# PEER block: the sums of gathered `u` rows written straight into the table of dots

## The reference, cut to what matters

```python
def block(args):
    xb, eb, gb = args
    u = u_tab[eb]
    act = jax.nn.gelu(jnp.einsum('thkd,td->thk', u, xb), approximate=False)
    return jnp.einsum('thk,thkd->td', gb * act, v_tab[eb])
```

## Time and profile before

| | |
|---|---|
| time, median of 3 runs | 2834.77 us (2832.07 to 2835.41) |
| span of the profiled execution | 2830.4 us |
| median less this span | 4.4 us |
| TensorE busy | 2757.7 us (97%) |
| VectorE busy | 2169.3 us (77%) |
| ScalarE busy | 1115.4 us (39%) |
| GpSimd busy | 1628.8 us (58%) |
| mean granted TensorE clock | 0.993 |

### The profile page before, as it was taken

The page is one execution under the profiler, slowest core; times in us unless marked ns, Lnnn a source line. Parts: engine busy times, 40 slices in busy tenths (PEclk is TensorE's granted clock), DMA queues, the critical chain, the costliest instruction groups (busy, mean ns, idle before and its releaser), DMA issues. The chain is left out here.

```text
span 2830.4 us, 47325 instructions
## 1 busy us (share of the span) xinstructions
PE 2757.7 (97%) x16000; PEld 1508.1 (53%) x16000; DVE 2169.3 (77%) x4268; ACT 1115.4 (39%) x1554; POOL 1628.8 (58%) x1485
## 2 busy tenths in 40 slices
PE   6999999999999999999999999999999999999998
PEld 3445754554666666656666665444444444444443
DVE  3998865322788999989999994777777777777778
ACT  4354554223444444446677664312211221222122
POOL 1331001111233444477777775888888898889884
PEclk9999999999999999999999999999999999999999
DMA  3231030111344555568888888899999999999995
GB/s 128 79 137 35 1 139 22 58 47 42 110 156 162 191 192 185 177 238 308 321 308 308 322 307 321 316 367 330 338 343 339 328 343 358 352 343 352 358 349 189
DMA packets 265252, 658.08 MB, mean 233 GB/s; under 512 B 17552, under 2 KB 116112, under 8 KB 261952
## 3 DMA queue, kind: packets, MB, share of 16 engines
q1 hardware_dynamic: 190992, 387.37, 38.2%
q0 software_dynamic: 74160, 269.52, 26.7%
HBM read 547.24 MB, written 110.10 MB: 232 GB/s over the span
## 5 line engine op out<-in xcount | busy, mean ns | idle before, releaser
L95 POOL TENSOR_TENSOR w_low<-w_ring,w_high 128x1024 f16<-128x1024 f32 x164 | 375.3, 2289 | 884.9 <-ACT w_ring L90 884.3
L1605 PE MATMUL psum<-region_y,w_high 128*128 128x384 f16 x2048 | 670.4, 327 | 10.8 <-issue 4.3
L1606 PE MATMUL psum<-region_y,w_high 128*128 128x384 f16 x2048 | 670.5, 327 | 0.0
L1607 PE MATMUL psum<-region_y,w_low 128*128 128x384 f16 x2048 | 670.4, 327 | 0.0
L2320 DVE TENSOR_TENSOR region_x<-region_x,psum 128x1024 f32<-128x1024 f32 x192 | 234.3, 1220 | 213.6 <-PE psum L2154 213.4
L2171 ACT ACTIVATE scores<-w_ring 128x1024 bf16<-128x1024 f32 x64 | 67.0, 1048 | 655.6 <-PE psum L2154 651.6
L2152 PE MATMUL psum<-scores,share 128*128 128x512 bf16 x752 | 286.0, 380 | 7.7 <-DVE region_x L2320 6.9
L2152 PE MATMUL psum<-scores,wh 128*128 128x512 bf16 x768 | 291.2, 379 | 1.4 <-POOL wl L2203 1.4
L2154 PE MATMUL psum<-scores,wl 128*128 128x512 bf16 x768 | 291.2, 379 | 0.0
L2153 PE MATMUL psum<-vl,wh 128*128 128x512 bf16 x768 | 291.2, 379 | 0.0
L1663 ACT ACTIVATE ge<-psum 128x384 f32<-128x384 f32 x256 | 124.9, 488 | 415.6 <-PE psum L1607 413.5
(11 more groups left out here) (306 smaller groups left out, 5478.3 us busy)
## 6 DMA issues: line engine op xcount, KB each, us to landing
w_ring<-in_u_t_dram SPq DMA_DIRECT2D x128, 512.0 KB, 6.1
acts_dram<-ge SPq DMA_DIRECT2D x128, 384.0 KB, 4.8
gates_dram<-scores SPq DMA_DIRECT2D x24, 2048.0 KB, 9.2
scores<-gates_dram SPq DMA_DIRECT2D x30, 1536.0 KB, 16.4
scores<-acts_dram SPq DMA_DIRECT2D x30, 1536.0 KB, 19.8
w_ring<-in_v_t_dram SPq DMA_DIRECT2D x64, 512.0 KB, 11.0
more_v<-in_v_t_dram SPq DMA_DIRECT2D x64, 512.0 KB, 4.9
w_ring<-in_w_stream_dram SPq DMA_DIRECT2D x20, 512.0 KB, 3.5
```

The lines of the kernel that those rows point to most:

```text
L95: pool.tensor_tensor(self.wl[:, s, :], self.wf[:, s, :], self.wh[:, s, :], ALU.subtract).then_inc(self.w_lo, 1)
L1605: pe.matmul(a, uh[:, par, row], xh[:, n, cols], start=(n == 0), stop=False)
L1606: pe.matmul(a, uh[:, par, row], xl[:, n, cols], start=False, stop=False)
L1607: last = pe.matmul(a, ul[:, par, row], xh[:, n, cols], start=False, stop=(n == KC - 1))
```

## The change

A take's sum now goes straight to its column in `dot`, in both stages. The small tables `dots`, the copies out of them, and the semaphore `dot_ok` with all its waits are gone. Who waited for `dot_ok` waits for something else: ScalarE at the switch for `row_used`, SyncE's load of `final_g` for `acc_ok`.

```diff
             def take(group, slot, seen, tile):
-                after(dve, dot_ok, group)
                 dve.wait_ge(row_in[slot], seen)
                 for j in range(SLOT_ROWS):
                     a = row[slot * SLOT_ROWS + j]
                     dve.scalar_tensor_tensor(out=a, in0=a, scalar=1.0, in1=xtok[tile], op0=ALU.mult, op1=ALU.mult,
-                                             accum_out=dots[:, j:j + 1]).then_inc(row_used, 1)
-                dve.wait_ge(row_used, SLOT_ROWS * group + SLOT_ROWS)
-                dve.tensor_copy(dot[:, tile, ds(SLOT_ROWS * group - SEL * tile, SLOT_ROWS)],
-                                dots[:, :]).then_inc(dot_ok, 1)
+                                             accum_out=dot[:, tile, ds(SLOT_ROWS * group + (j - SEL * tile), 1)]
+                                             ).then_inc(row_used, 1)
...
-            sp.wait_ge(dot_ok, GROUPS // 2)
+            sp.wait_ge(acc_ok, 3)
             sp.dma_start(xtok[:, :], final_g).then_inc(xtok_in, 16)
...
                     if at_switch(g) and (what, c) == ("v", CPG - 1):
-                        act.wait_ge(dot_ok, PHASE)
+                        act.wait_ge(row_used, used(PHASE, True))
                         act.activation(dot[:, 1, :], dot[:, 1, :], ACT.Gelu, scale=1.0 / XS).then_inc(gelu_ok, 1)
...
                 if kind == "u":
                     dve.scalar_tensor_tensor(out=row[j], in0=row[j], scalar=1.0, in1=acc[1], op0=ALU.mult,
-                                             op1=ALU.mult, accum_out=dots[:, k:k + 1]).then_inc(row_used, 1)
-                    if k == U_ONE - 1:
-                        dve.wait_ge(row_used, used(g, True) + U_ONE)
-                        dve.tensor_copy(dot[:, 1, ds(U_ONE * g + U_DONE, U_ONE)], dots[:, :]).then_inc(dot_ok, 1)
+                                             op1=ALU.mult, accum_out=dot[:, 1, ds(U_ONE * g + (U_DONE + k), 1)]
+                                             ).then_inc(row_used, 1)
...
             def add(g, of_u):
-                if of_u:
-                    after(dve, dot_ok, g)
                 for q in range(PAIRS):
```

More of the change, by code:

```diff
@@ L1462, in select_and_activate @@
     step_rows = sb(ctx, "u_step_rows", [P, RING, SLOT_ROWS], I32)
-    dots = sb(ctx, "u_dots", [P, SLOT_ROWS], F32)
     zero = sb(ctx, "u_zero", [P, 1], F32)
@@ L1467, in select_and_activate @@
     tok_in = sems("u_tok_in")
-    zero_ok, step_ok, row_used, dot_ok = (sems(f"u_{n}") for n in (
-        "zero_ok", "step_ok", "row_used", "dot_ok"))
+    zero_ok, step_ok, row_used = (sems(f"u_{n}") for n in ("zero_ok", "step_ok", "row_used"))
     rest = work[:, 0:HP * NK].rearrange("p (h n) -> p h n", h=HP)
@@ L2019, in combine @@
     step_rows = sb(ctx, "step_rows", [P, 2, BOTH], I32)
-    dots = sb(ctx, "dots", [P, U_ONE], F32)
     weight = sb(ctx, "weight", [P, GATHERED, SEL], F32)
@@ L2030, in combine @@
     row_in = [sems(f"row_in{j}") for j in range(BOTH)]
-    xtok_in, zero_ok, step_ok, row_used, dot_ok, gelu_ok, weight_ok, acc_ok = (sems(n) for n in (
-        "xtok_in", "zero_ok", "step_ok", "row_used", "dot_ok", "gelu_ok", "weight_ok", "acc_ok"))
+    xtok_in, zero_ok, step_ok, row_used, gelu_ok, weight_ok, acc_ok = (sems(n) for n in (
+        "xtok_in", "zero_ok", "step_ok", "row_used", "gelu_ok", "weight_ok", "acc_ok"))
     TILES = [*range(GATHERED, TB - 1), *range(GATHERED), TB - 1]
```

## The result

The changed kernel takes 2843.0 us (median of 5 runs, 2840.4 to 2846.2), the kernel before beside it 2833.4 us: a ratio of 1.0043, 95% interval 1.0032 to 1.0054. It is **slower by 9.6 us**; the prediction said 2844.1 us and +9.3. The profiled spans differ by 10.8 us, 2841.2 against 2830.4.

The account below looks back on a forecast made before the run. TensorE, busy 97% of the span, was taken as the bound, with GpSimd the second chain. Terms -0.5 - 0.2 + 8.0 + 2.0 = +9.3 us; 2839.7 + 4.4 gave 2844.1 us, range 2838 to 2849.

Parts of the forecast that it names:

- The switch, +8.0 and +2.0: Start of group 16: TensorE waits behind Gelu's later wait, +8.0 us, then loses +2.0 us at the low clock.
- Group 0 to 2, -0.2: Combine's start: group 0 ends 7.3 us earlier, but TensorE waits 5.1 us for GpSimd at group 2, clock 2.0: -0.2 us.
- Selection, -0.5: Selection stage: dropping 88 copies may shorten TensorE's wait for GpSimd at 1223 to 1227: -0.5 us, at most 6.7.
- The second half: From group 20: groups of 31.45 instead of 31.08 us cost 4.1 us; recurrence left open, 0 in the sum.
- rival (a): No change: clock stays up at both new waits, or second-half slide stays away; +5.3 or +5.2 us; chance 0.24.
- Rival (c): Slower still: GpSimd stays the bound from the switch, with longer low clock and slow additions; +12.8 us, chance 0.12.
- Rival (b): Faster: without copies GpSimd is early at 1223, groups 0 to 2 and the second half; -8.1 us, chance 0.04.

Follow-up runs that it names:

- the early Gelu: Changed kernel with ScalarE's Gelu at the switch waiting for the fifth take of group 15 (row_used 155), not the tenth: 2831.7 us, ratio 1.0003.
- The two runs with GpSimd's order: GpSimd's eight subtractions before its gathers in groups 2 to 5; changed kernel with Gelu waiting for row_used 155: 2826.4 us; kernel before: ratio 1.0003.
- the run of that part alone: Kernel before with the 88 copies of the selection stage left out and combine untouched: ratio 1.0003.
- GpSimd's small addition: Changed kernel, Gelu waiting for row_used 155, one of GpSimd's five small additions per group from group 1 on left out: 2826.2 us, ratio 0.9984.
- the maximum: Kernel before, with combine's copy of the dots written as a two-input maximum of the table with itself: ratio 0.9996.

## Why the prediction was right

The terms that carry the sum came out where and as predicted, but part of the nearness of +9.6 to +9.3 is luck: without the selection the terms add up to +9.8 against 9.73 in the inner length, with 1.05 us too little at the switch and 1.1 us too little gain in groups 0 to 2.

*The switch, +8.0 and +2.0.* Right in place, chain and size: 8.75 and 2.30. Five runs that change only where or for what the Gelu waits move it as the chain says: 0 for the fifth take, the eighth, and the Gelu placed behind; 4.3 for the ninth; 10.3 for the tenth, in the kernel before (waits and low clock together). ScalarE's idle time was 26.02 us where some 26 had been expected. Of the 0.75 that was missing, 0.5 is the pair of subtractions: I took 4.1 us, between 3.7 and 5.3, and it took 4.64 (2324.16 to 2328.80), beside a weighting that itself took 6.93 us.

*Group 0 to 2, -0.2.* Right in mechanism: group 0 -7.66 for -7.3, GpSimd's start of group 2 at 1860.07 for 1859.7, the wait of TensorE +4.97 for +5.1, the clock +1.36 for +2.0. That nets to -1.33 in the changed kernel's profile, not -0.2; more than half of the difference is the low clock, which varies by a microsecond between profiles. With the early Gelu the whole inner length shows -0.02. The two runs with GpSimd's order show both halves to be real.

*Selection, -0.5.* Its sign isn't shown. Group 0 starts 1.10 us later in the changed kernel's profile, but the profile was already 1.35 us behind at 705 us (a matmul at 704.31 before, at 705.66 after), ahead of the changed lines, and the run of that part alone shows no difference.

*The second half.* Right (0): the groups of 31.45 us are back, and they begin with one late gather, as the prediction read it. What it left open, whether that happens again, the profiles settle: the gather is late in all twelve that have GpSimd's small addition, whatever happens at the switch. So the single event was no ground for the weight that rival (a) took from it. Rival (c), GpSimd the bound from the switch on, did not come: TensorE's group 16, 2.3 us longer at the low clock, gave time to GpSimd, which was 2.96 us ahead at the start of group 17 and 0.76 at that of group 18, as in the kernel before. Of its terms the rows show the slower subtractions and 0.3 us of the longer low clock.

*Rival (b)* asked for a GpSimd that the copies held up. In group 0 the trace has it the other way round: GpSimd's subtractions ran at 2.11 to 2.14 and 1.62 to 1.65 us while the copy waited. By the Trainium skill (SBUF — State Buffer, Who interferes with whom) the first to issue keeps the shared ports for a whole instruction. The direction agrees with these rows. The length doesn't: the copy waited through five subtractions that began after it, and so did the maximum, which the Trainium skill counts as contending for its two SBUF inputs. Near 1227 a wait of TensorE did shrink without the copies, from 3.81 to 1.07 us, and came back as 3.39 at 1245.8, so that nothing measurable was gained there.

## What to carry to other kernels

When a signal is replaced by a count on another semaphore, work out which instruction gives that count and what that instruction waits for: here "all ten takes" instead of "the first five" tied a ScalarE wait to the end of TensorE's own group, with TensorE's next inputs queued behind it. Put an instruction that waits for something late behind whatever others need soon. And before a stall is booked as a gain, ask which other engine is late by as much; removing VectorE's stall alone gave 0 to 1.4 us, reordering GpSimd alone 0.2, and both 7.7 us.

## What the runs showed of the hardware

A VectorE operation of 128x5 elements with all its operands in SBUF waited 10.46 us through GpSimd's back-to-back subtractions, and 3.11 us when the run was parted. Copy or two-input maximum made no difference. Takes and adds with an input in PSUM ran beside the same subtractions at their usual 1.2 us. The four weightings of a group (768 columns each, both inputs in SBUF by the code), which met two subtractions in the changed kernel at the switch, took 6.93 us together instead of 3.56, and all of that is in the last two, which otherwise take 0.95 us each:

```profile
2324.43 2.88 DVE L317 TENSOR_TENSOR scores<-scores 128x768 f32<-128x768 f32 x1
```
```profile
2327.23 2.39 DVE L317 TENSOR_TENSOR scores<-scores 128x768 f32<-128x768 f32 x1
```

Each ends 0.8 us behind a subtraction (these end at 2326.5 and 2328.8), as if it had been held until then; and the second subtraction, which starts while the third weighting is still to be done, takes 2.34 us instead of 1.64. So a weighting got in between two subtractions that follow each other at once, where the small copy did not in a run of six. By what the copy was held across instructions, no run here tells.

The cost of the low clock (1.2 GHz) after a wait of TensorE hardly follows the wait: 1.7 us after 2.6 us of waiting, 1.3 to 2.6 us after 4.4 to 5.0 (seven profiles; 1.3 to 1.5 in four, 2.4 to 2.6 in three), 1.5 and 2.3 us after 8.75. Two profiles with equal waits can differ by a microsecond in this alone.
